# Attention on TensorE: the order of transposes, scores and outputs inside one piece

## The chip, the cores and the metric

One core of a Trainium2 chip. The time is device microseconds (us) for one execution of the whole program. Several executions are timed, and the median is compared.

## What is computed

The reference is one transformer block on 1024 tokens of width 1024: an input projection, a state-space mixer, two kinds of attention with six heads of 64 each, an output projection and a gated feed-forward layer. The change is in the attention:

```
# kind j = 0, dilated: three windows, (128, 1), (512, 4), (2048, 16), merged by their log-sums
# kind j = 1, forgetting: causal, with a bias from a running sum of log forget gates
s = einsum('bqhd,bkhd->bhqk', q, k)
p = softmax(where(valid, s + bias, -inf))
o = einsum('bhqk,bkhd->bqhd', p, v)
```

The kernel folds the three windows of the dilated kind into one causal pass: the bias `lnc` holds the logarithm of how many of the three patterns hold a pair of positions.

## The kernel before

The kernel is written engine by engine: each engine has its own instruction list, in an order written out by hand, and waits on semaphores. Before the attention stand the projections and the state-space mixer; behind it stand the output projection, the feed-forward products and the down projection, all bound to TensorE's list.

The attention runs over six pairs of heads i, and in each over the two kinds j. So there are twelve heads. A head has four units, one for each group g of 256 query rows (`QB` = 2 blocks r of 128 rows), in the order `ORDER = (3, 0, 2, 1)`. A row block (g, r) has (2g + r + 1) x 128 keys, from 128 to 1024. A unit has g + 1 pieces b, each of 256 keys. So a head has ten pieces, and its blocks go by TensorE, VectorE and ScalarE in these steps, whose short names are used below:

- S(g, r), `scores` (lines 2063 to 2082): query times key in two terms, high part (L2077) and low part (L2078), into the two PSUM banks of row r. For j = 1 one more small product (L2080) adds the causal mask. There is one pair of banks for each r, so `scores` waits until the exponential of the same r in the unit before has read them (`exp_done`).
- `row_max` on VectorE (L1429): adds the bias and takes the extreme of a row, then reads the accumulator (`nm`).
- `exp_row` on ScalarE (L961): exponential and row sum into `pr`, and then the read of its accumulator.
- T(g, b), `transposed` (lines 2084 to 2095, product L2093): three or four 128 x 128 blocks of `pr` are turned into one of two PSUM banks. For b = 0 it waits for both exponentials of its unit; and for the piece two before it to have left the bank (`pt_low_done`).
- `pt_high` on ScalarE (L971) copies the bank to `pth`, `pt_low` on VectorE (L1161, `ptl`) takes the rest.
- O(g, b), `outputs` (lines 2097 to 2115, L2112 and L2113): values times the turned probabilities, added up over the pieces of a unit. Once a unit, `y_back` (L2121) turns the sums back, and VectorE scales them into `ya`.

TensorE works ahead: in the body of a piece it issues the scores of the unit two ahead (one row block in each of the first two pieces) and the transposes of the piece two ahead. So the transposes of T(3, 0) and T(3, 1) of the next head stand in the body of unit g = 1, T(1, 0) and T(1, 1) in that of g = 2, and T(2, 0) in the last piece of g = 3. The scores S(3, r) of the next head stand in g = 2, its S(0, r) in g = 1, S(2, r) in g = 3 and S(1, r) in g = 0. ScalarE's order is in `act_unit`: `pt_high` of the piece two ahead, then `exp_row` of the unit two ahead. VectorE's is in `dve_unit`: `row_max` first, then `pt_low`, then the scaled output; `values_high` (L1414) closes a unit g = 3.

Of the kernel before, what the change touches and what calls it, by code (L numbers as in the profile page):

```python
# [105 lines left out]
def block_kernel(nc, x_t, x_tok, gains, gain_rows, w_u, w_f, w_v, w_stream, w_out, w_down, s_par, s_bc, rows,  # L106
# [5 lines left out]
    with ctx:  # L112
# [80 lines left out]
        def due(count):  # L193

            return not isinstance(count, int) or count > 0
# [557 lines left out]
        def group_at(a, b):  # L753
            return 2 * (4 * (a % 2) + b) + a // 2
# [10 lines left out]
        def piece(i, j, g, b):  # L765

            return i * (2 * PCS) + slot_of(j, g, b)

        def slot_of(j, g, b):

            return j * PCS + sum(f + 1 for f in ORDER[:PLACE[g]]) + b

        def unit(i, j, g):
            return i * (2 * UNITS) + (j * UNITS + PLACE[g])
# [24 lines left out]
        def probs(g, r):  # L799

            q_ = QB * g + r
            at = P * q_ * (q_ + 1) // 2
            return pr[:, at:at + width(g, r)]

        def parts_of(g, b):

            return [(a, r) for a in range(2) for r in range(QB) if b < g or r >= a]
# [1128 lines left out]
        def _(pe):  # L1936
# [53 lines left out]
            for a in range(4):  # L1990
                for b in range(4):
                    g = 4 * a + b
# [17 lines left out]
            for a in range(4):  # L2010
                for b in range(4):
                    g = group_at(a, b)
# [50 lines left out]
            def scores(i, j, g, r):  # L2063

                u, w = unit(i, j, g), width(g, r)
                if g == ORDER[0] and r == 0:

                    pe.wait_ge(staged[j], i * 80 + 80)

                if due(u * 2 + (r - 1)):  # L2070
                    pe.wait_ge(exp_done, u * 2 + (r - 1))
                qs = slice((QB * g + r) * P, (QB * g + r + 1) * P)
                for b in range(-(-w // HALF)):
                    n = min(HALF, w - b * HALF)
                    out, key = ps[:, 2 * r + b, 0:n], slice(b * HALF, b * HALF + n)
                    masked = j == 1 and b == (w - 1) // HALF
                    pe.matmul(out, qa[:, j, qs], ks[:, j, key], start=True, stop=False)  # L2077
                    last = pe.matmul(out, ql[:, j, qs], ks[:, j, key], start=False, stop=not masked)  # L2078
                    if masked:
                        last = pe.matmul(ps[:, 2 * r + b, n - P:n], ident_b[:], mask_b[:],  # L2080
                                         start=False, stop=True)
                last.then_inc(qk_done, 1)

            def transposed(i, j, g, b):

                pc, slot = piece(i, j, g, b), slot_of(j, g, b)
                if b == 0:
                    pe.wait_ge(exp_done, unit(i, j, g) * 2 + 2)

                if due(pc - 1):  # L2090
                    pe.wait_ge(pt_low_done, pc - 1)
                for n, (a, r) in enumerate(parts_of(g, b)):
                    last = pe.transpose(ps[:, 4 + slot % 2, n * P:(n + 1) * P],  # L2093
                                        probs(g, r)[:, (2 * b + a) * P:(2 * b + a + 1) * P], ident[:])
                last.then_inc(pt_mm, 1)

            def outputs(i, j, g, b):

                slot = slot_of(j, g, b)
                if b == 0:  # L2100

                    if due(unit(i, j, g) - 1):
                        pe.wait_ge(y_done, unit(i, j, g) - 1)
                    if g == ORDER[0]:

                        pe.wait_ge(values_low_done, i * 2 + (j + 1))
                pe.wait_ge(pt_low_done, piece(i, j, g, b) + 1)
                for a in range(2):
                    rows_ = [r for a_, r in parts_of(g, b) if a_ == a]
                    out = outputs_bank(g)[:, rows_[0] * P:QB * P]  # L2110
                    cols = slice(a * QB * P, (a * QB + len(rows_)) * P)
                    pe.matmul(out, vs[:, j, 2 * b + a, :], pth[:, slot % 4, cols], start=b == 0 and a == 0, stop=False)  # L2112
                    last = pe.matmul(out, vs[:, j, 2 * b + a, :], ptl[:, slot % 4, cols], start=False,  # L2113
                                     stop=b == g and a == 1)
                last.then_inc(pv_done, 1)

            def y_back(i, j, g):

                pe.wait_ge(ot_done, unit(i, j, g) + 1)
                for r in range(QB):  # L2120
                    last = pe.matmul(y_bank(g, r), ot[:, PLACE[g] % 2, r * P:(r + 1) * P], ident2[:], start=True, stop=True)  # L2121
                last.then_inc(yt_mm, 1)

            def pe_unit(i, j, g, ahead_, prev, on, last):
                for b in range(max(g + 1, QB)):
                    if b < QB and ahead_:
                        scores(*ahead_, b)
                    if b <= g and on[b]:
                        transposed(*on[b])
                    if b <= g:  # L2130
                        outputs(i, j, g, b)
                    if b == min(g, 1) and prev:
                        y_back(*prev)
# [5 lines left out]
            for n in range(2):  # L2139
                transposed(0, *PIECES[n])  # L2140
            bodies(pe, pe_unit)

            def ssm_transposed(n):
# [207 lines left out]
```

## Time and profile before

| what | value |
|---|---|
| median of three executions | 1286.44 us (1285.92 to 1292.03) |
| the profiled execution: its time | 1285.62 us |
| its span | 1283.9 us |
| TensorE, matmuls: busy | 1227.0 us, 96% of the span |
| VectorE / ScalarE / GpSimd busy | 732.8 / 486.4 / 393.3 us |
| stretch of the attention | about 272 to 483 us |

The span is what the trace shows of the execution; the time has 1.7 us around it. Times in the trace are microseconds from the span's start. The busy time of TensorE counts a matmul as busy while it is in the pipeline, so two that overlap are counted by the time that they cover together.

### The profile page before, as it was taken

The numbers are of one execution on the slowest core, as the hardware profiler recorded it, in microseconds if no ns is written. First come the engines' busy times: TensorE is split into PE (matmuls) and PEld (weight loads), VectorE is DVE, ScalarE is ACT, GpSimd is POOL, SyncE is SP. The second block draws the span as 40 slices with busy tenths as digits, with TensorE's granted clock in tenths as the row PEclk, the third lists the DMA queues.
The fourth block names the chain that finished last, engine by engine and source line by source line (L and its number), as shares of the span: only waits on it lengthen the run. The fifth ranks groups of instructions, "written<-read, shape, count | busy, mean of one in ns | idle before, by whom it ended". The sixth has DMA issues, their size and how long they took to land.

```text
span 1283.9 us, 18491 instructions
## 1 busy us (share of the span) xinstructions
PE 1227.0 (96%) x6468; PEld 1041.4 (81%) x6468; DVE 732.8 (57%) x1348; ACT 486.4 (38%) x942; POOL 393.3 (31%) x342
## 2 busy tenths in 40 slices
PE   7999999989999998999999999999999989999996
PEld 6998788878888886887888888888888778888885
DVE  4615392267877775675766556656556453333357
ACT  6513212357777773443423333333333222201212
POOL 0099131154555510001813233233233122202200
PEclk9999999999999998999999999999999999999998
DMA  9232342295655411223122122122121264330202
GB/s 353 67 99 82 133 120 96 99 313 112 148 147 146 94 23 66 83 79 134 60 88 88 61 98 96 51 98 98 49 98 65 82 262 164 132 131 14 118 33 99
DMA packets 48260, 140.57 MB, mean 109 GB/s; under 512 B 18454, under 2 KB 18502, under 8 KB 45500
## 3 DMA queue, kind: packets, MB, share of 16 engines
q1 hardware_dynamic: 42620, 122.10, 26.7%
q0 software_dynamic: 5296, 16.87, 6.9%
q10 hardware_dynamic: 288, 0.85, 0.2%
q8 instruction: 36, 0.59, 0.2%
q14 instruction: 20, 0.16, 0.0%
HBM read 103.53 MB, written 35.68 MB: 108 GB/s over the span
## 4 chain that ended last, share of the span: by engine, by line
PE 89%; DVE 3%; issue 3%; ACT 2%; DMA 1%; DVEq 0%; POOL 0%; SPq 0%; ACTq 0%
PE ps L2261 19%; PE ps L2241 9%; PE ps L2242 9%; PE ps L2240 9%; PE ps L2184 7%; PE ps L499 3%; PE ps L501 3%; PE ps L500 3%; PE ps L2093 3%; PE ps L1979 2%; PE ps L1978 2%; PE ps L1980 2%; PE ps L2077 2%; PE ps L2213 2%; PE ps L2215 2%
## 5 line engine op out<-in xcount | busy, mean ns | idle before, releaser
L1161 DVE TENSOR_TENSOR ev<-ps,ev 128x512 f32<-128x512 f32 x133 | 90.2, 690 | 116.1 <-PE ps L2242 116.1
L1161 DVE TENSOR_TENSOR z<-ps,z 128x512 f32<-128x512 f32 x80 | 51.6, 686 | 123.2 <-PE ps L2261 122.8
L2240 PE MATMUL ps<-t_hi,s_hi 128*128 128x512 f32 x304 | 118.3, 389 | 0.0
L2241 PE MATMUL ps<-t_lo,s_hi 128*128 128x512 f32 x304 | 118.3, 389 | 0.0
L2242 PE MATMUL ps<-t_hi,s_lo 128*128 128x512 f32 x304 | 118.3, 389 | 0.0
L1077 ACT ACTIVATE s_hi<-s_sum 128x512 fp32r<-128x512 f32 x72 | 45.6, 633 | 131.0 <-PE ps L2242 131.0
L1161 DVE TENSOR_TENSOR ptl<-ps,pth 128x512 fp32r<-128x512 f32 (+1 forms) x120 | 76.2, 636 | 30.8 <-ACT pth L971 28.4
L2240 PE MATMUL ps<-op_hi,s_hi 128*128 128x512 f32 x228 | 88.7, 389 | 0.0
L2241 PE MATMUL ps<-ol,s_hi 128*128 128x512 f32 x228 | 88.7, 389 | 0.0
L2242 PE MATMUL ps<-op_hi,s_lo 128*128 128x512 f32 x228 | 88.7, 389 | 0.0
L961 ACT ACTIVATE pr<-ps,nm 128x896 f32<-128x896 f32 (+3 forms) x96 | 71.2, 742 | 30.8 <-DVE nm L1429 29.9
L2093 PE MATMUL ps<-ident,pr 128*128 128x128 f32 x432 | 69.1, 279 | 12.2 <-ACT pr L961 11.6
L499 PE MATMUL ps<-op_hi,w_hi 128*128 128x512 f32 x192 | 75.3, 392 | 0.9 <-DVE fz L1307 0.9
L971 ACT ACTIVATE pth<-ps 128x512 fp32r<-128x512 f32 (+1 forms) x120 | 66.2, 552 | 23.1 <-PE ps L2093 22.7
L501 PE MATMUL ps<-op_hi,w_lo 128*128 128x512 f32 x192 | 74.7, 389 | 0.0
L500 PE MATMUL ps<-op_lo,w_hi 128*128 128x512 f32 x192 | 74.7, 389 | 0.0
L2112 PE MATMUL ps<-pth,vs 128*128 128x256 f32 x240 | 69.7, 312 | 0.9 <-DVE ya L1161 0.8
L1734 POOL TENSOR_TENSOR s_sum<-raw_b 128x512 f32<-128x512 f32 x18 | 30.3, 1684 | 125.9 <-DVE s_lo L1161 100.5
L2240 PEld LDWEIGHTS ps<-t_hi,s_hi 128*128 128x128 f32 x304 | 57.1, 188 | 11.9
L2241 PEld LDWEIGHTS ps<-t_lo,s_hi 128*128 128x128 f32 x304 | 57.1, 188 | 11.8
L2242 PEld LDWEIGHTS ps<-t_hi,s_lo 128*128 128x128 f32 x304 | 57.1, 188 | 11.8
L2261 PE MATMUL ps<-db_hi,hb_hi 128*128 128x512 f32 x192 | 59.8, 393 | 4.0 <-DVE hb_lo L1161 4.0
(318 smaller groups left out, 3209.6 us busy)
## 6 DMA issues: line engine op xcount, KB each, us to landing
hid_scratch<-hf SPq DMA_DIRECT2D x22, 512.0 KB, 2.9
w_raw<-w_stream SPq DMA_DIRECT2D x18, 512.0 KB, 4.0
raw_b<-w_stream SPq DMA_DIRECT2D x18, 512.0 KB, 5.0
qk_scratch<-qk_hi SPq DMA_DIRECT2D x12, 512.0 KB, 2.6
qk_scratch<-qk_lo SPq DMA_DIRECT2D x12, 512.0 KB, 2.9
qa<-qk_scratch POOLq DMA_DIRECT2D x24, 256.0 KB, 4.3
ks<-qk_scratch POOLq DMA_DIRECT2D x24, 256.0 KB, 5.5
hb_raw<-hid_scratch SPq DMA_DIRECT2D x3, 2048.0 KB, 7.3
```

The costliest lines, as they stand in the source:

```text
L499: e.matmul(out, w_hi[:, j, k, :], x_hi[:, k, half(h)], start=k == 0, stop=False)
L500: e.matmul(out, w_hi[:, j, k, :], x_lo[:, k, half(h)], start=False, stop=False)
L501: last = e.matmul(out, w_lo[:, j, k, :], x_hi[:, k, half(h)], start=False, stop=k == nk - 1)
L961: act.activation(probs(g, r), score_banks(r)[:, 0:width(g, r)], ACT.Exp, scale=-1.0, bias=nm[:, g, r:r + 1], accum_out=den[:, g, r:r + 1]) ...
L1161: return dve.tensor_tensor(out, a, b, op)
L2093: last = pe.transpose(ps[:, 4 + slot % 2, n * P:(n + 1) * P], probs(g, r)[:, (2 * b + a) * P:(2 * b + a + 1) * P], ident[:])
L2112: pe.matmul(out, vs[:, j, 2 * b + a, :], pth[:, slot % 4, cols], start=b == 0 and a == 0, stop=False)
L2184: last = pe.matmul(ps[:, 2 * (m % 2) + h, :], x[:, k, tok(m)], w[:, k, half(h)], start=first, stop=final)
L2240: pe.matmul(out, s_hi[:, j, k], x_hi[:, k, :], start=k == 0, stop=False)
L2241: pe.matmul(out, s_hi[:, j, k], x_lo[:, k, :], start=False, stop=False)
L2242: last = pe.matmul(out, s_lo[:, j, k], x_hi[:, k, :], start=False, stop=k == 3)
L2261: last = pe.matmul(ps[:, 4 + 2 * (m % 2) + b, :], x[:, k, tok(m)], w[:, k, half(b)], start=first, stop=final)
```

## The change

Inside the body of a piece, TensorE's list changes from scores, transposes, outputs to transposes, scores, outputs. No instruction is added or taken away, and no other engine's list is touched.

```
             def pe_unit(i, j, g, ahead_, prev, on, last):
                 for b in range(max(g + 1, QB)):
+                    if b <= g and on[b]:
+                        transposed(*on[b])
                     if b < QB and ahead_:
                         scores(*ahead_, b)
-                    if b <= g and on[b]:
-                        transposed(*on[b])
                     if b <= g:
                         outputs(i, j, g, b)
                     if b == min(g, 1) and prev:
                         y_back(*prev)
```

The two lists before and after, for one head (`|` parts the pieces; the names are those of above, and S(3), S(0), T(3) in the units g = 2 and g = 1 are the next head's):

```
before  g=3: S(2,0) T(3,2) O(3,0) | S(2,1) T(3,3) O(3,1) y_back | T(0,0) O(3,2) | T(2,0) O(3,3)
        g=0: S(1,0) T(2,1) O(0,0) y_back | S(1,1)
        g=2: S(3,0) T(2,2) O(2,0) | S(3,1) T(1,0) O(2,1) y_back | T(1,1) O(2,2)
        g=1: S(0,0) T(3,0) O(1,0) | S(0,1) T(3,1) O(1,1) y_back
after   g=3: T(3,2) S(2,0) O(3,0) | T(3,3) S(2,1) O(3,1) y_back | T(0,0) O(3,2) | T(2,0) O(3,3)
        g=0: T(2,1) S(1,0) O(0,0) y_back | S(1,1)
        g=2: T(2,2) S(3,0) O(2,0) | T(1,0) S(3,1) O(2,1) y_back | T(1,1) O(2,2)
        g=1: T(3,0) S(0,0) O(1,0) | T(3,1) S(0,1) O(1,1) y_back
```

## Rows read from the trace of the kernel before

**Rows 1.** Window view, steady attention: us, busy PE, PEld, DVE, ACT, POOL, clock, DMA.
```profile
308.00:476.00 168.00, 154.79 (x1193) 139.68 (x1192) 132.35 (x344) 126.54 (x298) 86.32 (x91) 1.00 0.49 118
```

**Rows 2.** Waits in the same stretch: waiter, releaser, us in total, times, longest.
```profile
DVE ptl L1161 <- ACT pth L971: 23.1, 34, 1.0
PE ps L2093 <- ACT pr L961: 9.8, 20, 0.6
PE ps L2077 <- ACT pr L961: 3.5, 9, 0.7
```

**Rows 3.** TensorE's timeline, an unmasked head (start, duration), from S(3, 0) to T(3, 0).
```profile
341.05 0.50 PE L2077 MATMUL ps<-ks,qa 128*128 128x512 f32 x1 [0.27 <-ACT pr L961]
...
341.98 0.49 PE L2093 MATMUL ps<-ident,pr 128*128 128x128 f32 x3
342.23 0.36 PE L2112 MATMUL ps<-pth,vs 128*128 128x256 f32 x1
342.43 0.28 PE L2113 MATMUL ps<-ptl,vs 128*128 128x256 f32 x1
...
342.79 0.39 PE L2077 MATMUL ps<-ks,qa 128*128 128x512 f32 x1
343.01 0.39 PE L2078 MATMUL ps<-ks,ql 128*128 128x512 f32 x1
...
346.76 0.65 PE L2093 MATMUL ps<-ident,pr 128*128 128x128 f32 x4 [0.62 <-ACT pr L961]
347.17 0.36 PE L2112 MATMUL ps<-pth,vs 128*128 128x256 f32 x1
...
347.73 0.28 PE L2077 MATMUL ps<-ks,qa 128*128 128x256 f32 x1
```

**Rows 4.** TensorE's timeline, the same head, on to the next head's S(3, 0).
```profile
347.97 0.60 PE L2093 MATMUL ps<-ident,pr 128*128 128x128 f32 x4
...
349.23 0.48 PE L2077 MATMUL ps<-ks,qa 128*128 128x512 f32 x1
349.54 0.39 PE L2078 MATMUL ps<-ks,ql 128*128 128x512 f32 x1
...
350.90 0.40 PE L2077 MATMUL ps<-ks,qa 128*128 128x512 f32 x1
...
354.16 0.65 PE L2093 MATMUL ps<-ident,pr 128*128 128x128 f32 x4 [0.40 <-ACT pr L961]
...
355.06 0.39 PE L2077 MATMUL ps<-ks,qa 128*128 128x384 f32 x1
...
357.86 0.50 PE L2077 MATMUL ps<-ks,qa 128*128 128x512 f32 x1 [0.42 <-ACT pr L961]
```

**Rows 5.** VectorE's timeline in that head: two score maxima, a low part, S(1, 0)'s maximum.
```profile
344.10 1.23 DVE L1429 CUSTOM_DVE_ANT_0 ps<-ps,lnc 128x1024 f32<-128x1024 f32 x1 [0.17 <-PE ps L2078]
...
351.24 0.69 DVE L1161 TENSOR_TENSOR ptl<-ps,pth 128x512 fp32r<-128x512 f32 x1
351.98 0.97 DVE L1429 CUSTOM_DVE_ANT_0 ps<-ps,lnc 128x768 f32<-128x768 f32 x1
...
356.50 0.55 DVE L1429 CUSTOM_DVE_ANT_0 ps<-ps,lnc 128x384 f32<-128x384 f32 x1
```

**Rows 6.** ScalarE's timeline: exponentials and their closing reads.
```profile
342.38 0.19 ACT L961 ACTIVATION_READ_ACCUMULATOR pr<-ps,nm 128x1 f32 x1
...
346.44 0.19 ACT L961 ACTIVATION_READ_ACCUMULATOR pr<-ps,nm 128x1 f32 x1
```

**Rows 7.** The masked head that follows: TensorE and one read of ScalarE.
```profile
359.04 0.19 ACT L961 ACTIVATION_READ_ACCUMULATOR pr<-ps,nm 128x1 f32 x1
359.66 0.40 PE L2077 MATMUL ps<-ks,qa 128*128 128x512 f32 x1
...
363.71 0.65 PE L2093 MATMUL ps<-ident,pr 128*128 128x128 f32 x4 [0.54 <-ACT pr L961]
...
375.00 0.50 PE L2077 MATMUL ps<-ks,qa 128*128 128x512 f32 x1 [0.27 <-ACT pr L961]
```

More of the change, by code:

```diff
@@ L2125, in pe_unit @@
                 for b in range(max(g + 1, QB)):
+                    if b <= g and on[b]:
+                        transposed(*on[b])
                     if b < QB and ahead_:
                         scores(*ahead_, b)
-                    if b <= g and on[b]:
-                        transposed(*on[b])
                     if b <= g:
```

## The prediction

> **What bounds the kernel now.** I read the page first: TensorE is busy 96% of the span. So a change in its order can give little or cost something, and what matters is where it idles in the attention and what ends those gaps. The window view of the steady stretch [rows 1] shows TensorE busy for 154.79 of 168 us at full clock (the granted clock is 1.00, the 2.4 GHz level), so 13.2 us of gaps; VectorE is at 79% and ScalarE at 75%. The view of waits names them [rows 2]: transposes wait 9.8 us in 20 gaps and scores 3.5 us in 9 gaps, all for ScalarE's exponentials. So each of the ten heads of that stretch has three gaps, and the time of a head is TensorE's own list plus these three.
>
> The timelines show which steps stand before them. In the unmasked head the gaps are before S(3,0) at 341.05 and T(3,0) at 346.76 [rows 3], and before T(2,0) at 354.16; then the next S(3,0) at 357.86 [rows 4]. So the head takes 357.86 - 341.05 = 16.81 us, and the masked one 375.00 - 357.86 = 17.14 us [rows 4, 7]. What ends each gap, followed back:
> - T(3,0) needs exp(3,1), whose closing read runs 346.44 to 346.63 and is followed 0.13 us later by the transpose [rows 3, 6]. That exponential follows row_max(3,1), which begins at 344.10 after waiting for S(3,1), issued at 342.79 [rows 3, 5]. So this gap moves with the issue of S(3,1). The chain view instead steps from this read to O(2,2), because ScalarE's queue had passed a wait on it ahead of time; I don't take that step, since the exponential was already running.
> - T(2,0) needs exp(2,1), from row_max(2,1) at 351.98, from S(2,1) issued at 350.90. row_max(2,1) also stands right behind the low part of 351.24 + 0.69 = 351.93 [rows 4, 5]: both of its feeders arrive almost together.
> - S(3,0) needs its banks from exp(1,0), which follows row_max(1,0) at 356.50 [rows 4, 5]. Ahead of that row_max VectorE has the low part of piece (2,0), the cast of the values and a reciprocal, all counted from T(2,0). So S(3,0) stands 357.86 - 354.16 = 3.70 us behind T(2,0) by way of VectorE, not TensorE.
>
> One loop runs through a head, then: S(3,0), S(3,1), exp(3,1), T(3,0), S(2,1), exp(2,1), T(2,0), exp(1,0), S(3,0). It passes TensorE's list in three places, and the change reorders two of them and a part of the third.
>
> **The change part by part.** Nothing is added: the same products, no DMA, no wait that wasn't there. What moves is seven score blocks a head by one transpose each (S(1,1) has none beside it). GpSimd's loads of the next queries and keys wait for the last scores of a head and are wanted a head later, and SyncE's bias row waits for row_max: both shift by under 1 us against 17 us, so at nothing.
>
> Step A, S(3,1) now behind T(1,0), and T(2,2) gone from in front of it. Before: S(3,0) 0.93, T(2,2) 0.25, O(2,0) 0.56, so S(3,1) at +1.74 [rows 3]. After: S(3,0) starts at the same time, as exp(1,0) sets it; T(2,2) has run in its gap (0.25 in a gap of 0.27 or 0.42). Then 0.93 and O(2,0) at 0.48 bring TensorE to T(1,0) at +1.41. But T(1,0) needs both exponentials of unit g = 1, and the read of exp(1,1) ends at 342.38 + 0.19 = 342.57 [rows 6]; with the 0.13 us of above it starts at 342.70, +1.65. It takes 0.41 after a wait (346.76 to 347.17 [rows 3]), so S(3,1) stands at +2.06: +0.32 us. In the masked head the read ends at 359.23 [rows 7], the transpose can start at 359.36, TensorE arrives then, and S(3,1) goes from 359.66 to some 359.75: +0.09 us. This is where the gain of T(2,2) in the gap goes.
>
> Step B, S(0,0) behind T(3,0). Before, S(0,0) ran in the gap ahead of T(3,0), for nothing. After, it runs behind it. It costs what S(0,1)'s two products of twice the columns take, 347.97 - 347.73 = 0.24 us [rows 3, 4], since short products go at nearly one pace; 0.30 with the mask product (an estimate).
>
> Step C, S(2,1) behind T(3,3): three blocks of transposes, 342.23 - 341.98 = 0.25 us as for T(2,2) [rows 3]. The moves of T(3,1) and T(3,2) past S(0,1) and S(2,0) change nothing in front of S(2,1), which had both ahead of it already. VectorE could hide it only if row_max(2,1) waited for VectorE alone; but the low part ahead of it waits for row_max(2,0), and S(2,0) moves too, by S(0,0) and T(3,2), so both feeders come later by about 0.5 us.
>
> Step D, joints. The first output product behind a transpose takes 0.20 us to the next (342.23 to 342.43), the other three 0.36 together, 0.12 each; the first score product behind y_back takes 0.31, against 0.22 behind an output product (349.23 and 342.79) [rows 3, 4]. No row has scores behind a transpose, so I take the same 0.08 for it, with 0 and 0.16 as ends. Then y_back, T(3,2), S(2,0), O(3,0) has one such joint where there were two (-0.08), and the ends of S(3,1) and S(2,1) move by 0.08 each: +0.08 a head.
>
> Step E, T(2,1) ahead of S(1,0), but row_max(1,0) waits for VectorE. S(1,0) stood 355.06 - 354.16 = 0.90 behind T(2,0); with at most 0.41 for T(2,1) it starts at 1.31, and by the wider pair at 342.79 (0.22 to the second product, 0.39 for that) it has ended by 1.92. Some 0.2 us on, VectorE can start (an estimate; its idle time at 344.10, 0.17 us, was of this kind). It started at 356.50 - 354.16 = 2.34 [rows 3 to 5]. Cover: 0.22 us. I take nothing.
>
> A head thus costs 0.32 + 0.24 + 0.25 + 0.08 = 0.89 us (dilated) or 0.09 + 0.30 + 0.25 + 0.08 = 0.72 us (forgetting). Scores of the next head exist for eleven heads: five dilated and six forgetting receive A and B, so 5 x 0.89 + 6 x 0.72 = 8.8 us, and the first has step C alone, 0.25. The sum is +9.0 us. The profiled execution took 1285.62 us, 0.8 below the median, so 1294.6 against it and 1286.44 + 9.0 = 1295.4 against the median. The stages behind are TensorE's own list and begin later by as much.
>
> Steps A and B rest on TensorE not running later products past a waiting transpose. In the trace, O(1,0) ran at 347.17, behind the T(3,0) that had waited [rows 3], though its own inputs, made by VectorE before 346 us, were there.
> The Trainium skill, page "TensorE: Matmul & The Clock Gate", section "Step-by-step: what each phase is for", says that this engine's queue may draw weight loads forward but that matmuls stay in program order. The trace agrees at that place. Were products drawn forward too, step B would cost nothing and the sum would be some 3.0 us lower, about 1292.4.
>
> **The rivals.**
> *No loss, the delays are absorbed.* If VectorE's feeders and not the scores bound both maxima, A and C vanish and B alone stays: 5 x 0.24 + 6 x 0.30 = 3.0 us, 1289.4. For it: VectorE's 79% and the feeder at 351.93. Against: row_max(3,1) has 0.17 us of idle time ahead of it that a score product ended [rows 5].
> *Faster, earlier transposes feed the copies.* VectorE waits 23.1 us for ScalarE's high parts [rows 2]. With transposes first, the high parts come earlier by the score block that stood in front, up to 0.93 us [rows 3]; if that brought VectorE to row_max(1,0) and the others earlier, the gaps before S(3,0) and T(2,0) would close, by 0.4 + 0.4 us a head less B's 0.27: 0.53 x 12 = 6.4 us, or some 1280. It decides if T(2,0) or exp(3,1) moves forward. Against: T(2,0)'s place isn't touched, and both lists put row_max ahead of the low part.
> *Heavier, S(1,0) becomes a feeder.* T(2,1) needs its bank back from VectorE. The cover of 0.22 us in step E decides: if T(2,1) starts over 0.22 us late, S(3,0) moves too. Late by 0.7 us, 0.5 us a head would come on top, 6 us in all, 1301.4.
>
> **How the numbers follow.** Forecast 0.64, absorbed 0.22, heavier 0.09, faster 0.05. The measurement tells about 0.5% (6.4 us) from nothing. The forecast's own spread is 1291.5 to 1299 (joints 0 or 0.16, A at half or full), of which 0.04 lies within 0.5% of before. So faster 0.05, same 0.22 + 0.04 = 0.26, slower 0.60 + 0.09 = 0.69. The range 1288 to 1300 holds the forecast, most of the absorbed case and part of the heavier, and leaves out the faster one.
>
> **What would show it.** Right: the gap before S(3,0) is 0.2 us or less with T(2,2) in it; the gap before T(3,0) is longer, about 1.4 us in unmasked heads, with S(0,0) behind it; S(3,1) starts some 2.06 us behind S(3,0); T(3,0) to T(2,0) grows from 7.40 by about 0.55; T(2,0) to S(3,0) stays at 3.70; a pair of heads takes 35.5 us, not 33.95. TensorE's busy time is as before. Wrong: a pair at 34.5 or less (something I call a feeder wasn't one), or T(2,0) to S(3,0) above 3.9 (step E costs).

## The result: slower by 0.7%

The changed kernel takes 1297.19 us (median of four, 1296.29 to 1297.71) against 1286.86 us (four executions of before). The ratio is 1.0071, with a 95% interval of 1.0044 to 1.0099, so +9.1 us with 5.7 to 12.7; the medians differ by 10.3 us. Forecast were 1295.4 us and +9.0 us.

TensorE's busy time on the page of the profile after is 1230.4 us, where it was 1227.0:

```profile
span 1294.6 us, 18491 instructions
PE 1230.4 (95%) x6468; PEld 1044.0 (81%) x6468; DVE 730.5 (56%) x1348; ACT 484.5 (37%) x942; POOL 393.8 (30%) x342
```

The work is the same and the span 10.7 us longer, so most of the time went into gaps. Not all of it: from the second head's S(3,0) to the last head's, ten heads, the length grew from 170.32 to 179.41 us and TensorE's busy time from 156.61 to 159.16. So 6.5 us of the 9.1 are gaps, and the other 2.6 are the same products covering more time.

```profile
289.71:460.03 170.32, 156.61 (x1201) 140.99 (x1201) 134.76 (x351) 127.58 (x300) 86.77 (x95) 1.00 0.53 125
```

```profile
292.13:471.54 179.41, 159.16 (x1200) 142.38 (x1201) 133.05 (x351) 125.96 (x300) 86.90 (x95) 1.00 0.51 119
```

The window view of the changed kernel over the same 168 us of attention answers to [rows 1] (us, then busy of PE, PEld, DVE, ACT, POOL, granted clock, DMA share, GB/s), and its view of waits to [rows 2]:

```profile
308.00:476.00 168.00, 149.64 (x1128) 133.71 (x1127) 125.30 (x329) 117.94 (x281) 86.41 (x91) 1.00 0.49 118
```

```profile
ACT pr L961 <- DVE nm L1429: 44.0, 75, 1.1
PE ps L2093 <- ACT pr L961: 17.7, 18, 1.3
DVE ps L1429 <- PE ps L2080: 12.5, 31, 0.8
DVE ps L1429 <- PE ps L2078: 8.4, 20, 0.6
...
PE ps L2077 <- ACT pr L961: 0.2, 1, 0.2
```

TensorE's gaps grew from 13.2 to 18.4 us. The change did what it says: scores hardly wait for exponentials any more (0.2 us, where it was 3.5), since T(2,2) fills that gap. But transposes wait 17.7 us instead of 9.8. And the row maxima of VectorE wait for score products for 12.5 + 8.4 us, where it was 6.0 + 3.0: the engine that feeds the exponentials gets its scores later.

TensorE's timeline of the changed kernel over an unmasked head (start, duration) answers to [rows 3] and [rows 4]:

```profile
346.18 0.50 PE L2077 MATMUL ps<-ks,qa 128*128 128x512 f32 x1
...
347.89 0.65 PE L2093 MATMUL ps<-ident,pr 128*128 128x128 f32 x4
348.30 0.48 PE L2077 MATMUL ps<-ks,qa 128*128 128x512 f32 x1
348.61 0.40 PE L2078 MATMUL ps<-ks,ql 128*128 128x512 f32 x1
...
352.36 0.65 PE L2093 MATMUL ps<-ident,pr 128*128 128x128 f32 x4 [1.28 <-ACT pr L961]
352.76 0.31 PE L2077 MATMUL ps<-ks,qa 128*128 128x128 f32 x1
...
356.68 0.49 PE L2093 MATMUL ps<-ident,pr 128*128 128x128 f32 x3
356.92 0.48 PE L2077 MATMUL ps<-ks,qa 128*128 128x512 f32 x1
357.24 0.40 PE L2078 MATMUL ps<-ks,ql 128*128 128x512 f32 x1
...
360.27 0.65 PE L2093 MATMUL ps<-ident,pr 128*128 128x128 f32 x4 [0.73 <-ACT pr L961]
...
363.38 0.49 PE L2093 MATMUL ps<-ident,pr 128*128 128x128 f32 x3
363.96 0.50 PE L2077 MATMUL ps<-ks,qa 128*128 128x512 f32 x1
```

S(3,0) at 346.18 is followed by T(1,0) at 347.89, which had to wait for exp(1,1), and only then by S(3,1), 2.12 us behind S(3,0). T(3,0) comes at 352.36 after a gap of 1.28 us, with S(0,0) behind it. T(3,3) at 356.68 stands ahead of S(2,1), and T(2,0) waits 0.73 us. The next S(3,0) comes at 363.96: 3.69 us behind T(2,0), as before. T(2,2) at 363.38 sits in the old gap in front of it.

Distances of this kind are the measure of all that follows. From the fourth to the tenth head, heads of one kind repeat within 0.06 us in one execution (0.09 in one of the runs), while the time of a whole execution scatters by several us. The first, second, third and eleventh heads differ from them, the second by up to 0.9 us. They are read in every run from the same two heads, the fifth (unmasked, dilated) and the sixth (masked, forgetting), counted from the head's S(3,0), in us; "head" is the distance to the next S(3,0), and "first" the length of the first head. Each kernel has one profiled execution; the kernels are described below.

| kernel | S(3,1) | T(3,0) | S(2,1) | T(2,0) | head | masked: S(3,1) | T(3,0) | S(2,1) | T(2,0) | head | first |
|---|---|---|---|---|---|---|---|---|---|---|---|
| before | 1.74 | 5.71 | 9.85 | 13.11 | 16.81 | 1.80 | 5.85 | 10.10 | 13.45 | 17.14 | 17.29 |
| after | 2.12 | 6.18 | 10.74 | 14.09 | 17.78 | 1.91 | 6.04 | 10.89 | 14.31 | 18.01 | 19.20 |
| g = 2 alone | 2.06 | 6.11 | 10.26 | 13.52 | 17.22 | 1.91 | 6.03 | 10.28 | 13.63 | 17.32 | 17.56 |
| g = 1 alone | 1.72 | 5.70 | 10.05 | 13.31 | 17.01 | 1.80 | 5.85 | 10.45 | 13.78 | 17.48 | 17.74 |
| g = 3 alone | 1.72 | 5.70 | 10.10 | 13.44 | 17.14 | 1.80 | 5.84 | 10.35 | 13.77 | 17.47 | 19.29 |
| g = 0 alone | 1.72 | 5.72 | 9.87 | 13.13 | 16.83 | 1.80 | 5.84 | 10.10 | 13.45 | 17.14 | 16.87 |
| T(2,2) alone | 1.57 | 5.66 | 9.81 | 13.07 | 16.77 | 1.53 | 5.58 | 9.83 | 13.18 | 16.87 | 18.53 |
| T(3,2) alone | 1.72 | 5.69 | 9.84 | 13.18 | 16.88 | 1.79 | 5.84 | 10.10 | 13.47 | 17.17 | 18.70 |
| O(1,0) first | 1.72 | – | 9.67 | 12.93 | 16.63 | 1.79 | – | 9.81 | 13.15 | 16.85 | 18.12 |
| both fills | 1.58 | – | 9.62 | 12.88 | 16.58 | 1.52 | – | 9.67 | 13.00 | 16.70 | 16.91 |
| after, first head old | 2.11 | 6.17 | 10.72 | 14.07 | 17.77 | 1.90 | 6.03 | 10.88 | 14.29 | 17.98 | 20.55 |
| four free swaps | 1.64 | 5.74 | 9.83 | 13.21 | 16.91 | 1.53 | 5.58 | 9.87 | 13.25 | 16.94 | 18.37 |
| both fills, cast late | 1.76 | – | 9.81 | 13.07 | 16.43 | 1.76 | – | 9.90 | 13.24 | 16.76 | 17.18 |
| cast late | 1.91 | 5.99 | 10.14 | 13.41 | 16.77 | 1.80 | 5.91 | 10.17 | 13.51 | 16.87 | 17.46 |

A dash: the transpose had no gap of its own in front of it. From the first S(3,0) to the last `y_back` the attention took 211.3 us before and 223.3 after, +11.9 us: 1.9 in the first head, 9.1 in the next ten, 0.9 in the last. The rest of the two executions differs the other way by 1.7 us (800.2 and 798.4 us behind the attention). Nothing that was changed runs there, and the runs below have 798.1 to 800.0, so that is scatter between executions.

### The profile page after: what moved, and what is told of

It reads as the page before. It is cut to its first block, busy times and chain, and to the rows that moved or that the text cites. A ratio compares the mean times of both kernels' runs of the same rounds, so it can differ in the third digit from the quotient of the medians.

```text
span 1294.6 us, 18491 instructions
## 1 busy us (share of the span) xinstructions
PE 1230.4 (95%) x6468; PEld 1044.0 (81%) x6468; DVE 730.5 (56%) x1348; ACT 484.5 (37%) x942; POOL 393.8 (30%) x342
## 3 DMA queue, kind: packets, MB, share of 16 engines
q0 software_dynamic: 5296, 16.87, 6.9%
## 4 chain that ended last, share of the span: by engine, by line
PE 90%; DVE 4%; issue 3%; ACT 2%; DMA 0%; DVEq 0%; ACTq 0%; SPq 0%
PE ps L2261 19%; PE ps L2240 9%; PE ps L2242 9%; PE ps L2241 9%; PE ps L2184 7%; PE ps L499 3%; PE ps L501 3%; PE ps L500 3%; PE ps L2093 3%; PE ps L2077 2%; PE ps L1979 2%; PE ps L1978 2%; PE ps L1980 2%; PE ps L2213 2%; PE ps L2215 2%
## 5 line engine op out<-in xcount | busy, mean ns | idle before, releaser
L2093 PEld LDWEIGHTS ps<-ident,pr 128*128 128x128 f32 x432 | 49.3, 147 | 30.7 <-DVE ptl L1161 20.2
```

## Experiments

The theory: one loop sets a head's time (S(3,0), S(3,1), exp(3,1), T(3,0), S(2,1), exp(2,1), T(2,0), exp(1,0), S(3,0)), and a swap costs only where it delays one of its scores. Two rivals: every swap costs the same, by slower joints (places where a product of one kind follows one of another); or the transposes' waits for both exponentials carry it all.

**One unit at a time.** Each kernel is before with the new order in one kind of unit. For g = 2 the edit is this, and the others differ in the number:

```
                 for b in range(max(g + 1, QB)):
+                    first = g == 2
+                    if first and b <= g and on[b]:
+                        transposed(*on[b])
                     if b < QB and ahead_:
                         scores(*ahead_, b)
-                    if b <= g and on[b]:
+                    if not first and b <= g and on[b]:
                         transposed(*on[b])
```

> The new order in the units g = 2 alone: T(2,2) ahead of S(3,0), T(1,0) ahead of S(3,1); all else as before. Loop theory (only scores that feed the next awaited exponential count): S(3,1) starts 2.1 us behind S(3,0) instead of 1.74 in unmasked heads and 1.9 instead of 1.80 in masked ones, T(3,0) later by as much, all other distances as before: 5 x 0.47 + 6 x 0.19 = +3.5 us. Rival, joints (every swap costs the same, because products behind a transpose start slower; 10.3 us over 79 swaps, 0.13 each): 22 swaps, +2.9 us, but the distance from S(3,0) to S(3,1) grows by only 0.26. Rival, waits (the transposes' waits for both exponentials carry it all, half here and half in g = 1): +5 us.

Measured: 1288.65 us, ratio 1.0024 (1.0009 to 1.0038), +3.1 us. S(3,1) at 2.06 and 1.91, and the head 0.41 and 0.18 us longer, which with 5 and 6 heads is +3.1 us. Its timeline shows why S(3,1) is late:

```profile
342.54 0.50 PE L2077 MATMUL ps<-ks,qa 128*128 128x512 f32 x1
...
343.47 0.37 PE L2112 MATMUL ps<-pth,vs 128*128 128x256 f32 x1
...
344.19 0.65 PE L2093 MATMUL ps<-ident,pr 128*128 128x128 f32 x4
344.60 0.47 PE L2077 MATMUL ps<-ks,qa 128*128 128x512 f32 x1
```

The transpose stands 1.65 us behind S(3,0), the start that step A gave it, and S(3,1) 0.41 behind that. With all seven swaps they stand at 1.71 and 2.12: there the closing read of exp(1,1) ends 0.06 us later, as it does with g = 0 alone, so T(2,1) ahead of S(1,0) moves S(3,1) by that much, through T(1,0), in unmasked heads.

> The new order in the units g = 1 alone: T(3,0) ahead of S(0,0), T(3,1) ahead of S(0,1). Loop theory: T(3,0) starts where it did, S(0,0) behind it costs 0.24 to 0.30 us from T(3,0) to S(2,1), and nothing else: +3.0 us. Joints: 22 swaps, +2.9 us. Waits: +5 us.

Measured: 1290.69 us, 1.0042 (1.0023 to 1.0061), +5.4 us. The heads say less, +0.20 and +0.34, so 5 x 0.20 + 6 x 0.34 = +3.0 us, which is at the interval's lower end (+3.0). T(3,0) starts where it did, 5.70, and the cost arises between it and S(2,1).

> The new order in the units g = 3 alone: T(3,2) ahead of S(2,0), T(3,3) ahead of S(2,1). Loop theory: S(2,1) starts 0.17 us later behind T(3,0) (the three blocks of T(3,3) less one joint) and ends 0.25 later, and T(2,0) with it: 12 x 0.25 = +3.0 us. Joints: 24 swaps, +3.1 us. Waits: no transpose here waits for an exponential, so 0 us.

Measured: 1290.58 us, 1.0025 (1.0006 to 1.0045), +3.2 us by the ratio. Heads +0.33 and +0.33, 11 x 0.33 = +3.6 us, and the first head is 2.0 us longer. S(2,1) starts 0.25 us later and its second product, like T(2,0), 0.33 later. That is three blocks of T(3,3) at 0.11 us each, as the account of step D below works out. With no transpose waiting for an exponential in these units, the rival of waits is out.

> The new order in the units g = 0 alone: T(2,1) ahead of S(1,0). Loop theory: VectorE, not S(1,0), sets row_max(1,0), so T(2,0) to S(3,0) stays 3.70 us: 0 us. Joints: 12 swaps, +1.6 us. Waits: 0 us. If S(1,0) is a feeder after all, S(3,0) comes later and it costs up to 0.4 x 12 = 4.8 us.

Measured: 1286.36 us, 1.0006 (0.9986 to 1.0026). Heads +0.02 and 0.00. So the rival of joints is out as well by the distances: twelve swaps for nothing. (The interval of the time, -1.8 to +3.3 us, would not tell 0 from its 1.6.) In its timeline S(1,0) is 1.31 us behind T(2,0) instead of 0.90, and the next S(3,0) at 3.70 all the same:

```profile
354.80 0.65 PE L2093 MATMUL ps<-ident,pr 128*128 128x128 f32 x4 [0.40 <-ACT pr L961]
355.70 0.65 PE L2093 MATMUL ps<-ident,pr 128*128 128x128 f32 x4
356.11 0.42 PE L2077 MATMUL ps<-ks,qa 128*128 128x384 f32 x1
...
358.50 0.50 PE L2077 MATMUL ps<-ks,qa 128*128 128x512 f32 x1 [0.42 <-ACT pr L961]
```

The four add up: 0.41 + 0.20 + 0.33 + 0.02 = 0.96 us in the unmasked head, where all together gave 0.97; 0.18 + 0.34 + 0.33 = 0.85 in the masked one, where it was 0.87.

**Filling a gap without delaying a feeder.** T(2,2) alone ahead of its scores (`first = g == 2 and b == 0`):

> The order before, with one swap only: T(2,2) ahead of S(3,0), in the gap that was there. Loop theory: S(3,0) starts at the same place, O(2,0) follows it at once, and S(3,1) starts when exp(1,1) has left its banks: 1.58 us behind S(3,0) instead of 1.74 (unmasked) and about 1.47 instead of 1.80 (masked). row_max(3,1) must also wait for the low part of (2,2), which leaves a gain of 0.13 and 0.20 us: 5 x 0.13 + 6 x 0.20 = -1.9 us. Joints theory (a swap costs 0.13 wherever it stands): +1.4 us.

Measured: 1283.60 us, 0.9969 (0.9951 to 0.9987), -4.0 us. S(3,1) at 1.57 and 1.53, as forecast to 0.06; heads -0.04 and -0.27, so 5 x 0.04 + 6 x 0.27 = -1.8 us. The sum is the forecast one, its split (0.13 and 0.20) is not. The gain that the change looks for exists, and T(1,0) in the same unit takes it away: by difference to g = 2 alone, T(1,0) costs 0.45 us in heads of both kinds.

O(1,0) moved ahead of T(3,0), into the other gap:

```
                     if b < QB and ahead_:
                         scores(*ahead_, b)
+                    if g == 1 and b == 0:
+                        outputs(i, j, g, b)
                     if b <= g and on[b]:
                         transposed(*on[b])
-                    if b <= g:
+                    if b <= g and not (g == 1 and b == 0):
                         outputs(i, j, g, b)
```

> The order before, with O(1,0) ahead of T(3,0), so that it fills the gap in front of T(3,0); no swap of scores and transposes. Loop theory: T(3,0) starts where it did, S(2,0) and S(2,1) come up to 0.56 us earlier behind it, and VectorE's list (row_max(2,0) behind the scaled output and the reciprocal) takes back about half: some 0.3 us a head, 11 x 0.3 = -3.3 us, between -2 and -5. If the gap in front of T(3,0) were TensorE's own business (dispatch, weights) and not exp(3,1): 0 us.

Measured: 1283.80 us, 0.9980 (0.9953 to 1.0006), not clear of no change. The heads are clear: -0.18 and -0.29, so 5 x 0.18 + 6 x 0.29 = -2.6 us.

> Both of these together: T(2,2) ahead of S(3,0) and O(1,0) ahead of T(3,0). Loop theory: they act in different parts of the loop and add up, -1.9 - 3.3 = -5.2 us, which would be below the kernel before. If another engine becomes the bound of the loop, less than the sum: about -3 us.

Measured: 1282.73 us, 0.9974 (0.9952 to 0.9996), below before. Heads -0.23 and -0.44: -3.8 us, near the sum of the two (-4.4), less than forecast. TensorE is busy for 161 of the 168 us, and a new small wait has come, for the scaled output of VectorE:

```profile
308.00:476.00 168.00, 160.95 (x1208) 142.59 (x1207) 134.30 (x352) 127.89 (x304) 86.68 (x92) 1.00 0.50 118
```

```profile
PE ps L2093 <- ACT pr L961: 4.0, 10, 0.4
PE ps L2112 <- DVE ya L1161: 1.8, 6, 0.8
```

**Which swap of g = 3.** T(3,2) alone (`first = g == 3 and b == 0`):

> The order before, with T(3,2) ahead of S(2,0) only; S(2,1) keeps its place behind the same products. Loop theory as predicted (S(2,1) alone feeds, a joint less): 0 us a head. With VectorE as second feeder (S(2,0) 0.36 later, row_max(2,0) and the low part behind it 0.2 later, row_max(2,1) with them): 11 x 0.2 = +2.2 us. On top, in both, the first head: there T(3,2) waits for VectorE's first low parts and now holds S(2,0) behind it, which in the run with both swaps of g = 3 made the first head 2.0 us longer: about +1.9 us.

Measured: 1286.95 us, 0.9990 (0.9976 to 1.0003). Heads +0.07 and +0.03: VectorE's other feeder takes next to nothing, and T(3,3) carries the cost of the unit. row_max(2,1) starts 1.35 us behind row_max(2,0) here, as little as in any run, so in this kernel it does wait for VectorE's own list. The first head is 1.4 us longer.

**Four swaps that should be free.** T(2,2), T(2,1), T(3,2) and T(3,1) ahead of their scores; T(1,0), T(3,0) and T(3,3) behind them (`first = (g, b) in ((2, 0), (0, 0), (3, 0), (1, 1))`):

> Four of the seven swaps: T(2,2) ahead of S(3,0), T(2,1) ahead of S(1,0), T(3,2) ahead of S(2,0), T(3,1) ahead of S(0,1); the other three (T(1,0), T(3,0), T(3,3)) stay behind their scores. Loop theory: the three left out carry all of the steady cost, so heads take 16.8 us (unmasked: -0.04 for T(2,2), +0.03 for T(3,2)) and 16.9 (masked: -0.27 + 0.03), a pair 33.7 and not 35.8; the first head about 1.5 to 1.9 us longer by T(3,2). In all 5 x 0 - 6 x 0.24 + 1.7 = about 0 us against before. Rival (every swap costs its share): 4 of 7 of the loss, a pair of 35.0 us, +6 us.

Measured: 1286.81 us, 1.0013 (0.9992 to 1.0035). A pair of heads takes 16.91 + 16.94 = 33.85 us, against 33.95 before and 35.79 with all seven. So the three left out carry the steady loss, whole. T(3,1) wasn't run alone: the other three of these four sum to -0.19 us a pair and the four measure -0.10, so it can cost about 0.1 us a pair at most.

**The first head.** The first head of the changed kernel is 1.9 us longer, where step C alone gave 0.25. The changed order everywhere but in the first head's unit g = 3 (`first = not (isinstance(i, int) and i == 0 and j == 0 and g == 3)`):

> The changed kernel's order everywhere but in the first head's unit g = 3, which keeps the order before (S(2,0) ahead of T(3,2), S(2,1) ahead of T(3,3)). Theory: the changed kernel's first head is 1.9 us too long because T(3,2) waits there for VectorE's first low part and holds S(2,0) behind it, while TensorE's clock is at the lower level. Expected: first head 17.3 us and not 19.2, all later heads as in the changed kernel (17.78 and 18.01 us); attention 1.9 us shorter than in the changed kernel, so some +8.5 to +10 us against before. Rival (the long first head comes from when the first loads land, not from the order): first head stays at 19 us.

Measured: 1296.48 us, 1.0078 (1.0040 to 1.0116). The later heads are as expected, but the first missed: it took 20.55 us. VectorE's timelines around it are first of before, then of the changed kernel, then of this one:

```profile
282.41 0.83 DVE L1429 CUSTOM_DVE_ANT_0 ps<-ps,lnc 128x640 f32<-128x640 f32 x1 [1.45 <-issue]
...
283.76 0.96 DVE L1429 CUSTOM_DVE_ANT_0 ps<-ps,lnc 128x768 f32<-128x768 f32 x1
```

```profile
283.82 0.83 DVE L1429 CUSTOM_DVE_ANT_0 ps<-ps,lnc 128x640 f32<-128x640 f32 x1 [2.35 <-DMA qk_scratch<-qk_lo]
286.17 0.97 DVE L1429 CUSTOM_DVE_ANT_0 ps<-ps,lnc 128x768 f32<-128x768 f32 x1 [0.91 <-PE ps L2078]
```

```profile
284.06 0.83 DVE L1429 CUSTOM_DVE_ANT_0 ps<-ps,lnc 128x640 f32<-128x640 f32 x1 [2.43 <-issue]
285.41 0.96 DVE L1429 CUSTOM_DVE_ANT_0 ps<-ps,lnc 128x768 f32<-128x768 f32 x1
```

What the order does there is plain. T(3,2) waits for VectorE's first low part, and S(2,0), which ran ahead of it and inside that wait, now comes behind it. First of before, then of the changed kernel:

```profile
278.57 0.78 PE L2077 MATMUL ps<-ks,qa 128*128 128x512 f32 x1
...
280.42 1.12 PE L2093 MATMUL ps<-ident,pr 128*128 128x128 f32 x4 [0.32 <-DVE ptl L1161]
```

```profile
280.92 1.11 PE L2093 MATMUL ps<-ident,pr 128*128 128x128 f32 x4 [1.44 <-DVE ptl L1161]
281.69 0.77 PE L2077 MATMUL ps<-ks,qa 128*128 128x512 f32 x1
```

In the four kernels with T(3,2) first, S(2,0) stands 8.8 to 9.1 us behind the head's S(3,0), and in the ten others 6.1 to 7.1. What this costs isn't separated from two other things.

The first is a load. row_max(2,0) waits in the first head for the last queries and keys to land in memory (VectorE waits for `qk_out` there). Counted from the first S(3,0), it starts at 9.99 us before, 10.89 after and 10.97 here, and anywhere from 9.6 to 11.2 in the other runs. That part is not shown to belong to the order. From row_max(2,0) to row_max(2,1) it is 1.35, 2.35 and again 1.35 us, so up to 1.0 us of the 1.9 is the late S(2,0) and S(2,1). But this distance is 1.48 to 2.76 us in the four kernels with T(3,2) first, and 1.83 us with g = 2 alone, where it isn't first.

The second is TensorE's clock. Its mean from 280 to 284 us was 0.50 in the changed kernel and 0.78 before. The two executions in which it stayed at 1.00 through the first head, g = 0 alone and both fills, have the shortest first heads, 16.87 and 16.91 us. Of the 3.3 us by which this run's first head is longer than the one before, 2.3 stand between T(2,0), at 287.50, and the next S(3,0): 6.14 us where it was 3.85. TensorE had waited 1.93 us in front of 285.64 and 0.87 in front of 287.50, and from 288 to 292 the granted clock was at the lower level, 1.2 GHz, with TensorE busy throughout:

```profile
284.00:288.00 4.00, 1.49 (x10) 1.32 (x11) 2.92 (x7) 2.63 (x6) 0.00 (x0) 0.84 1.04 372
288.00:292.00 4.00, 4.00 (x20) 4.00 (x20) 2.42 (x7) 1.83 (x4) 1.27 (x1) 0.50 0.52 209
```

**Who sets S(3,0).** The loop theory says VectorE's list does, the cast of the values (L1414) included. The edit in `dve_unit` moves that cast by one unit:

```
-                if g == ORDER[0] and not (last and j == 1):
+                if g == ORDER[1] and not (last and j == 1):
                     values_high(*((i, 1) if j == 0 else (i + 1, 0)))
```

> The kernel before with only the cast of the next values one unit later on VectorE; TensorE's order is untouched. Loop theory: T(2,0) to S(3,0) goes from 3.70 to 3.37 us in unmasked heads, where TensorE's list takes 3.28, and to about 3.45 where S(1,1) is masked; 12 x 0.3 = -3.6 us. Rival (TensorE's list sets it): 0 us, 3.70 stays.

Measured: 1283.79 us, 0.9978 (0.9961 to 0.9995), -2.8 us. T(2,0) to S(3,0) is now 3.36 us in both heads, so VectorE did set it:

```profile
353.89 0.65 PE L2093 MATMUL ps<-ident,pr 128*128 128x128 f32 x4 [0.39 <-ACT pr L961]
354.79 0.39 PE L2077 MATMUL ps<-ks,qa 128*128 128x384 f32 x1
356.45 0.47 PE L2077 MATMUL ps<-ks,qa 128*128 128x512 f32 x1
357.25 0.50 PE L2077 MATMUL ps<-ks,qa 128*128 128x512 f32 x1
```

But the heads are only 0.04 and 0.27 us shorter: 0.34 us is gained there, and in the unmasked head nearly all of it is given back, as S(3,1) now stands at 1.91 instead of 1.74, waiting for exp(1,1), whose closing read ends 0.05 us before it.

> The order with T(2,2) ahead of S(3,0) and O(1,0) ahead of T(3,0), and on VectorE the cast of the next values one unit later (end of g = 0, where VectorE waits for scores anyway, instead of the end of g = 3). Loop theory: from T(2,0) to S(3,0) the path is VectorE's (low part, cast, reciprocal, row_max(1,0)), 3.70 us; without the cast it is 3.37, but TensorE's own list there takes 3.53 us with T(2,2), so 0.15 us a head are gained: 12 x 0.15 = 1.8 us below the kernel without this edit, some -5 to -6 us against before. Rival (S(3,0) is set by TensorE's list or by S(1,0), not by VectorE): no difference from the kernel without it, -3.3 us.

Measured: 1283.55 us, 0.9975 (0.9957 to 0.9993). Heads 16.43 and 16.76, a pair 33.19 against 33.28 without the cast: no further gain that the times can tell. The unmasked head gains the 0.15 us that were forecast and the masked one loses 0.06. S(3,1) stands at 1.76 again, where the fills alone had 1.58 and 1.52: it waits for exp(1,1), as in the run before this one.

## Why the prediction was right, and where its terms were off

The forecast case came in: slower by the delays of S(3,1), S(0,0) and S(2,1). That +9.1 us meets +9.0 so closely is luck. The interval is 5.7 to 12.7 us, and the traces show the attention 11.9 us longer, against 9.0 forecast for it: 10.0 in the eleven heads behind the first (8.8 forecast) and 1.9 in the first (0.25). The rest of the two executions differs by 1.7 us the other way.

- The loop and its feeders hold. Delays made in separate units add up to the whole within 0.01 us in the unmasked head and 0.02 in the masked one, and leaving out just T(1,0), T(3,0) and T(3,3) removed all of the steady loss. My hand choice against the chain view was right too: S(3,1) later by 0.32 us alone moved T(3,0) by 0.40.
- Step A: 0.40 and 0.17 us forecast with its joint, 0.41 and 0.18 measured alone. The wait of T(1,0) for exp(1,1) was seen at the start computed for it.
- Step B: 0.24 and 0.30 us forecast, 0.20 and 0.34 measured. The reason given for 0.24, that short products go at nearly one pace, holds for S(0,0)'s pair, whose two products are 0.11 apart at 345.76 in the trace before, but not in general: the two of 128 columns in S(2,0) are 0.06 apart.
- Step C with its joint: 0.25 forecast (0.25 + 0.08 - 0.08), 0.33 measured in both kinds.
- Step D is the term that was misread, and it took the 0.08 us off step C. It read the 0.20 or 0.31 us behind a transpose as 0.08 us of extra time. But the first product behind a transpose is recorded 0.03 us after the last transpose's start, where two transposes stand 0.11 apart. So the 0.08 is only moved from one distance to the next. The trace before shows it on four and on three blocks:

```profile
343.71 0.60 PE L2093 MATMUL ps<-ident,pr 128*128 128x128 f32 x4
344.06 0.36 PE L2112 MATMUL ps<-pth,vs 128*128 128x256 f32 x1
344.27 0.28 PE L2113 MATMUL ps<-ptl,vs 128*128 128x256 f32 x1
...
345.01 0.50 PE L2093 MATMUL ps<-ident,pr 128*128 128x128 f32 x3
345.26 0.36 PE L2112 MATMUL ps<-pth,vs 128*128 128x256 f32 x1
345.46 0.28 PE L2113 MATMUL ps<-ptl,vs 128*128 128x256 f32 x1
```

  To the second output product it is 0.56 and 0.45 us; less 0.12 for the first one, four blocks take 0.44 and three 0.33. Scores behind T(3,3) in the changed kernel say the same: 357.24 - 356.68 = 0.56, less 0.23 is 0.33. So step C is 0.33 and not 0.25, with no joint to take off, and step A's 0.08 is right in size: T(1,0) takes 0.49 us behind its wait, not the 0.41 to the recorded start of the next product. The 0.08 us that are missing a head make 0.9 us in eleven.
- In masked heads, 0.72 forecast and 0.87 measured, 0.04 more comes from step B. A mask product ahead of an output product takes 0.12 us, and step B had allowed 0.06:

```profile
370.67 0.23 PE L2080 MATMUL ps<-mask_b,ident_b 128*128 128x128 bf16 x1
370.71 0.36 PE L2112 MATMUL ps<-pth,vs 128*128 128x256 f32 x1
370.91 0.28 PE L2113 MATMUL ps<-ptl,vs 128*128 128x256 f32 x1
```

  (370.91 - 370.67 = 0.24, less 0.12 for the output product.) Unmasked heads were 0.89 forecast and 0.97 measured.
- Step E: 0 forecast, 0.02 and 0 measured; S(1,0) started at the 1.31 us given as the bound. Its one effect, exp(1,1) later by 0.06 us, had no place in the sum.
- The first head was forecast at +0.25 and came at +1.9. Step C counted the products there and not the wait at their head: T(3,2) had to wait for VectorE, and S(2,0), which used to run in that wait, was behind it. That is the mechanism of step B, in a place where I had not looked for it. Up to 1.0 us of the 1.9 goes that way; how much is the order's, the load's or the clock's isn't settled.
- The sign "TensorE's busy time is as before" did not quite hold: 2.6 us more in ten heads.
- The stated spread of the forecast, 1291.5 to 1299, doesn't follow from its bracket. Joints of 0 or 0.16 move the sum by 0.9 us either way and half of step A takes 1.1 off, which gives 1293.4 to 1296.3. The attention's 11.9 us lie above that.
- The rivals: "absorbed" is out. In the changed kernel row_max(3,1) waits 0.64 us for scores in the unmasked head, and row_max(2,1) starts 1.55 us behind row_max(2,0), where VectorE's own list allows 1.35. "Faster" is out as well, T(2,0) and exp(3,1) didn't move forward. T(2,2) by itself does gain, but by an earlier S(3,1) and not through the copies. "Heavier" did not occur, S(1,0) stayed inside its cover.

The Trainium skill, page "TensorE: Matmul & The Clock Gate", section "Step-by-step: what each phase is for", has the matmuls stay in program order. The runs agree: with g = 1 alone changed, S(0,0) ran 0.41 us behind the start of the waiting T(3,0) and cost its 0.20 to 0.34 us a head. Before, it had run ahead of that wait, so its inputs were there.

## What to carry to other kernels

On an engine with one ordered list, put what feeds the next awaited result first and what is only consumed later behind it; ready work belongs into a gap only if the gap's own instruction was late anyway and nothing that feeds the loop is pushed back. Take such a swap apart by place: of seven swaps here one gained, three were nearly free (0.07 us or less for two of them, about 0.1 us a pair of heads at most for T(3,1)) and three lost, and the loss of the three hid the gain of the one. Read the distances inside the repeated body, which here hold to 0.1 us, before trusting times that scatter by several us; and look at the first and last turn by themselves, since a wait that is over in the steady state may be open there.

## What the runs showed of the hardware

The recorded start of a product of TensorE can mislead where its kind changes; read over two distances. In the trace before, from 308 to 476 us at a granted clock of 1.00, two transposes of 128 columns stand 0.11 us apart on average, two output products of 256 columns 0.12, and two score products of 512 columns 0.23. The first output product behind a transpose is recorded 0.03 us behind it and is followed after 0.20: 0.23 in all, which is 0.11 + 0.12. With g = 3 alone changed, scores of 512 columns have 0.03 + 0.32 behind a transpose, 0.345 in all, where 0.11 + 0.23 is 0.34. So going from transposes to either kind costs nothing that shows. Other changes of kind do cost something. Scores behind y_back have 0.08 + 0.31 = 0.40 us, some 0.05 more than 0.11 + 0.23. A score product of 128 columns takes 0.06 us ahead of another one but 0.11 ahead of a transpose. And a mask product takes 0.07 us ahead of a transpose but 0.12 ahead of an output product (0.04 + 0.20, less 0.12). What causes them isn't shown.
